# Two transformer models in a row: block 1's three in-layer norms without the sixteen idle products that TensorE issues in each

## The reference

```python
mod = silu(c) @ w_mod[l] + b_mod[l]
sh1, sc1, gt1, sh2, sc2, gt2 = jnp.split(mod, 6, axis=-1)
h = rms_norm(x, g_norm_mix[l]) * (1.0 + sc1) + sh1
x = x + gt1 * (attention(h @ w_in[l]) @ w_out[l])
h = rms_norm(x, g_norm_mlp[l]) * (1.0 + sc2) + sh2
x = x + gt2 * (jnp.square(jax.nn.relu(h @ w_mlp_in[l])) @ w_mlp_out[l])
```

## Time and profile before

| | us |
|---|---|
| median of 3 runs | 1664.45 (1663.45 to 1664.75) |
| the profiled execution's own time | 1665.32 |
| its span, from the first to the last instruction | 1663.4 |
| TensorE busy in the span | 1629.1 (98%) |
| VectorE busy | 1248.5 (75%) |
| ScalarE busy | 982.6 (59%) |

### The profile page before, as it was taken

How to read it: one execution, slowest core, us unless ns; L and a number is a source line. 1 busy time by engine, 2 the same in 40 slices (tenths; PEclk the granted TensorE clock), 3 DMA queues, 4 the chain that set the end, 5 groups by cost and what they waited for, 6 DMA issues and landing times.

```text
span 1663.4 us, 25160 instructions
## 1 busy us (share of the span) xinstructions
PE 1629.1 (98%) x9473; PEld 1364.3 (82%) x9473; DVE 1248.5 (75%) x1639; ACT 982.6 (59%) x1350; POOL 87.8 (5%) x105
## 2 busy tenths in 40 slices
PE   8999999999999999999999999999999999999998
PEld 6767888877777888899988888899978787887876
DVE  3876988877778665568676666568589988899887
ACT  4675544466754444546655545546667777677774
POOL 2150000004300000000000000000000000000000
PEclk9999999999999999999999999999999999999999
DMA  9757788845548565644355655554348999999995
GB/s 344 248 186 268 254 294 288 269 157 170 212 158 295 180 201 177 199 152 152 102 196 184 195 184 196 183 152 138 127 155 292 343 345 336 337 318 346 346 333 164
DMA packets 263287, 381.58 MB, mean 229 GB/s; under 512 B 8299, under 2 KB 197025, under 8 KB 263186
## 3 DMA queue, kind: packets, MB, share of 16 engines
q1 hardware_dynamic: 261520, 377.26, 68.5%
q0 software_dynamic: 1104, 1.76, 0.4%
q10 hardware_dynamic: 562, 1.18, 0.2%
HBM read 379.12 MB, written 1.05 MB: 229 GB/s over the span
## 4 chain that ended last, share of the span: by engine, by line
PE 82%; DVE 10%; ACT 4%; issue 1%; POOL 1%; DMA 1%; SPq 1%; DVEq 0%; ACTq 0%
PE bank L2285 55%; PE bank L2327 10%; PE bank L2329 5%; DVE w_low L1321 4%; ACT w_high L681 3%; PE bank L2375 3%; DVE mod_sums L1443 1%; PE bank L2884 1%; PE bank L2423 1%; DMA raw<-in_w_in_dram 1%; PE bank L2634 1%; SPq L462 1%; PE bank L2662 1%; DVE turned L1406 1%; DVE h_high_and_low L1391 0%
## 5 line engine op out<-in xcount | busy, mean ns | idle before, releaser
L1321 DVE TENSOR_TENSOR w_low<-raw,w_high 128x2048 fp32r<-128x2048 f32 (+2 forms) x315 | 689.4, 2192 | 178.7 <-ACT w_high L681 177.3
L681 ACT ACTIVATE w_high<-raw 128x2048 fp32r<-128x2048 f32 (+3 forms) x333 | 596.4, 1797 | 180.1 <-PE bank L2285 179.3
L2285 PE MATMUL bank<-w_high,h_high_and_low 128*128 128x512 f32 (+2 forms) x1536 | 485.3, 386 | 7.7 <-DVE w_low L1321 6.2
L2285 PEld LDWEIGHTS bank<-w_high,h_high_and_low 128*128 128x128 f32 x1536 | 285.4, 188 | 70.7 <-DVE w_low L1321 13.1
L2285 PE MATMUL bank<-w_low,h_high_and_low 128*128 128x512 f32 (+2 forms) x768 | 291.5, 380 | 0.0
L2327 PE MATMUL bank<-h_high_and_low,w_high 128*128 128x512 f32 x864 | 221.0, 394 | 2.9 <-DVE turned L2029 1.4
L2285 PE MATMUL bank<-w_high,act_high 128*128 128x512 f32 x544 | 213.6, 393 | 3.3 <-DVE act_low L1787 2.1
L2285 PE MATMUL bank<-w_low,act_high 128*128 128x512 f32 x544 | 211.6, 389 | 0.0
L2285 PE MATMUL bank<-w_high,act_low 128*128 128x512 f32 x544 | 211.2, 388 | 0.0
L2327 PEld LDWEIGHTS bank<-h_high_and_low,w_high 128*128 128x128 f32 x864 | 155.7, 188 | 33.9 <-issue 5.1
L2285 PEld LDWEIGHTS bank<-w_low,h_high_and_low 128*128 128x128 f32 x768 | 144.7, 188 | 24.0
(11 more groups left out here) (352 smaller groups left out, 1760.9 us busy)
## 6 DMA issues: line engine op xcount, KB each, us to landing
raw<-in_w_gu_exp_dram SPq DMA_DIRECT2D x160, 512.0 KB, 5.7
raw<-in_w_in_dram SPq DMA_DIRECT2D x52, 1024.0 KB, 5.3
raw<-in_w_mod_dram SPq DMA_DIRECT2D x48, 1024.0 KB, 5.5
raw<-in_w_dn_exp_dram SPq DMA_DIRECT2D x40, 1024.0 KB, 6.7
raw<-in_w_mlp_in_dram SPq DMA_DIRECT2D x32, 1024.0 KB, 5.6
raw<-in_w_mlp_out_dram SPq DMA_DIRECT2D x32, 1024.0 KB, 5.0
raw<-in_w_gu_dense_dram SPq DMA_DIRECT2D x22, 1024.0 KB, 5.1
raw<-in_w_out_dram SPq DMA_DIRECT2D x16, 1024.0 KB, 5.2
```

What stands on the lines that cost most here:

```text
L681: return nc.scalar.activation(dst, src, ACT.Copy, scale=scale)
L1321: V.tensor_tensor(wlo[w % SPLIT][:, 0:n], raw[raw_of(w) % RAW][:, 0:n], whi[w % SPLIT][:, 0:n].bitcast(F32), ALU.subtract).then_inc(raw_us ...
L2285: ins = T.matmul(out, lhsT, rhs, start=start and i == 0, stop=stop and i == len(pairs) - 1)
```

## The change

Eight lines of `turn_x` change: the choice of the idle bank and the three calls of `keep_busy`, for 2 + 2 + 5 + 7 = 16 products in each of norms 1, 2 and 3, are taken out. The transposes, their waits and `spread_rs` stay as they were and in their order. Norm 0 had no idle products here, since the calls stood behind `if n`. No other engine's list is touched.

```diff
         def turn_x(n, w, begin=0):
-            idle_bank = 7 if n % 2 else 4
             for i in range(begin, 4):
                 turn_quarter(n, i)
-                if n and i in (1, 2):
-                    keep_busy(2, idle_bank, w)
             if n:
-                keep_busy(5, idle_bank, w)
                 spread_rs(n)
-                keep_busy(7, idle_bank, w)
```

## The result

The changed kernel takes 1666.97 us in the median of 22 runs (1665.04 to 1668.86), and the kernel before, measured beside it, 1664.76 us (22 runs, 1663.19 to 1665.15). The ratio is 1.0015 with a 95% interval of 1.0009 to 1.0020: slower by 2.2 us. That is surely above nothing and just inside the 0.2% that the prediction had called the limit of what can be told from no change. The spread of its runs has grown too, from 2.0 to 3.8 us.

A forecast was written before the change was run, and what follows sets the result against it. TensorE was taken as the bound, busy 1629.1 of 1663.4 us. Gain 0, plus 1.15 us each in norms 1 and 3 and 1.45 in norm 2, made +3.75 us: median 1668.2, range 1667.0 to 1670.0 (8 in 10: 1663.8 to 1671.5).

The forecast's parts named there:

- The direct gain: Idle products of the three norms: removing them gains between 0 and 0.63 us; taken as 0.
- The clock falls in all three norms: New TensorE gaps of 1.6 and 2.25 us in each norm lower the clock; 2.5 to 5.5 us lost, chance 0.45.
- Rival 1: The clock holds through the norms' gaps: price 0, gain up to 0.63 us, 1663.8 to 1664.5 us; chance 0.25.
- rival 3: The clock stays down long, as over broken work at the start: 5.5 to 11.4 us lost; chance 0.11.
- rival 4: TensorE's queue was late after all and the spread comes sooner: near 1661 us; chance 0.02.
- How long it is down behind the restart: Once dense work begins again after a norm, the clock stays down 3.9 us; lower end near 1, upper 9 us.
- What that costs in norms 1 and 3: First products behind these norms: half of 3.9 us less 0.8 us slack, 1.15 us each.
- the slack: Time TensorE already loses waiting for the vector engine: 0.8 us behind norms 1 and 3, 0.5 us behind norm 2.
- Norm 2: First tile's products behind this norm: half of 3.9 us less 0.5 us slack, 1.45 us, all reaching the end.
- The spread at half rate: The spread's two transposes in each norm may run at half rate: up to 0.2 us a norm, taken as 0.
- rival 2: The clock falls in one or two norms, or rises again soon: 0.5 to 2.5 us lost; chance 0.17.

The follow-up runs named there:

- the transposes: Kernel before with the idle products of all three norms replaced by idle transposes of about the same time (5, 5, 12, 17): 1664.95 us, ratio 0.9999.
- the single removals: Kernel before with the sixteen idle products taken out of norm 1, 2 or 3 alone: 1665.88, 1665.68 and 1665.74 us.
- 21 idle products: Kernel before with 21 idle products instead of seven behind each spread: 1668.59 us, +3.76; behind norm 2's spread alone: 1665.41 us, +0.58.

## Why the prediction was right, and where it was off

- **The direct gain is nil: right.** The spread and the first product stand 0.06 and 0.14 us behind the vector engine's results, as they did. The work that hid the 48 products was the chain of squares, roots and first rests, and it is there without them.
- **The clock falls in all three norms: right.** PEclk was at 0.50 behind each, in the profile of the changed kernel. Rival 1, the clock holds, is out; so are rival 3 (in norms 1 and 3 the clock was back before the dense part) and rival 4. That the fall is the cause and not a bystander is shown by the transposes: they too take the idle products out, hold the clock, and cost nothing. It is shown a second time by the rows behind the restart, where a block takes 1.28 us while the clock is down and 0.70 us from 170.78 on, with the first product no later than before.
- **How long it is down behind the restart: near the mean, and partly by luck.** The forecast said 3.9 us, from the one rise at the start of the trace, which came under other work. It was 5.1 us in norm 1 (165.58 to about 170.7), 4.3 in norm 2 and 3.5 in norm 3 of one execution, and 6.1 in norm 2 of another. One value could at best be their mean.
- **What that costs in norms 1 and 3: right in the mean.** A block takes 1.28 us instead of 0.70, so 1 - 0.70/1.28 = 45% of the time at half rate is lost, less the slack. Norm 1: 5.1 x 0.45 - 0.84 = 1.5, measured 1.56 us. Norm 3: 3.5 x 0.45 - 0.84 = 0.7, measured 0.78 us. The forecast had 1.15 us for each; their mean was 1.17. By the medians of the single removals it was 0.99 and 0.85 us.
- **Norm 2 was mis-sized, and that is the step of the sum that failed.** The forecast took a slack of 0.5 us from the first tile's products and then said that "behind the norms TensorE is the bound, so what it loses there goes to the end". Behind norm 2 that is not so. In the kernel before, TensorE waits there for line 1321 at 367.15, and its products at 362.60 are stretched as well (0.73 us for two, where 0.54 is usual):

```profile
362.60 0.73 PE L2285 MATMUL bank<-w_high,h_high_and_low 128*128 128x416 f32 x2
...
367.15 0.53 PE L2285 MATMUL bank<-w_high,h_high_and_low 128*128 128x512 f32 x1 [0.49 <-DVE w_low L1321]
367.51 0.40 PE L2285 MATMUL bank<-w_low,h_high_and_low 128*128 128x512 f32 x1
```

In the changed kernel the same two places are these rows. TensorE comes later, finds the weights ready and waits for nothing:

```profile
365.05 0.54 PE L2285 MATMUL bank<-w_high,h_high_and_low 128*128 128x416 f32 x2
...
368.45 0.58 PE L2285 MATMUL bank<-w_high,h_high_and_low 128*128 128x416 f32 x2
368.87 0.40 PE L2285 MATMUL bank<-w_low,h_high_and_low 128*128 128x512 f32 x1
```

Counted from the spread, the pair of products is (365.05 - 354.84) - (362.60 - 353.86) = 1.47 us late, which is the forecast's 1.45. But the product at 367.51 is only (368.87 - 354.84) - (367.51 - 353.86) = 0.38 us late, and it stays so up to norm 3. So the loss in the first products was sized right, and 1.1 us of it were taken back where TensorE had waited anyway, which the forecast had left out: 0.49 us by the wait for line 1321, the rest at products that had stood further apart before, with no releaser named. With 21 idle products norm 2 forgave 2.48 - 0.63 = 1.85 us in all, not 0.5. Its term was thus 0.40 us in this profile, where the forecast had 1.45; in the kernel without norm 2's products alone it was 1.13 us in the profile and 0.79 in the median. In the profile this one term explains the step down from 3.75: the forecast's sum with 0.40 in it is 2.70, the marks give 2.74. The medians leave part of the step open. By the single removals norm 2 brings 0.66 us of the distance from 3.75 to 2.6, norms 1 and 3 bring 0.16 and 0.30, and intervals of 1.5 us to either side don't separate these.

- **The spread at half rate** was put at 0. It does happen where the fall comes early: 0.58 us in place of 0.43 in norm 2 of the changed kernel. It costs 0.15 us there.
- **The chances.** The measured 1666.97 us lies in the range for 8 in 10, and inside 0.2% of the kernel before, to which the prediction gave 0.54. The forecast itself had 2.5 to 5.5 us, and the +2.2 us lies just under it, in the range that rival 2 had by number. Rival 2's mechanism, a fall in one or two norms or an early rise, is not what the profile shows: the clock fell in all three and was down behind the restart for 4.3 us in the mean. The time also follows the clock from run to run: of the 22 runs of the changed kernel the nine with a mean granted clock of 0.994 took 1668.0 us in the mean, the six with 0.995 took 1666.8, and the seven with 0.996 took 1666.0. How long the half rate lasts and how much of it falls on wanted work differ from run to run, and with them the time.

What stays open is why the clock held in norm 1 with the nine idle products ahead of the spread and not in norms 2 and 3 of the same execution. Where the fall lies within a norm changes from execution to execution, and no run here sets it.

## What to carry to other kernels

A product that does nothing is free where TensorE waits anyway, and what it buys is read from the granted clock behind the wait, not from its busy time: look at PEclk, and at the distance between the first products after the restart. Put the idle work last, right ahead of the wanted work: seven products there did as well as sixteen as far as these runs can tell, while nine ahead of the spread lay 0.94 us above the kernel before, with a fall in two norms (its interval takes in no change too). Where the clock fell all the same, the half rate was spent wholly or in part on the seven. And price a delay by what waits behind it: about the same 2.4 us cost 1.5 us behind a norm that only TensorE bounds and 0.6 us behind one whose weights come late as well.

## What the runs showed of the hardware

- In the second profile of the kernel with seven products the clock fell in all three norms, and the mean granted clock of the execution was 0.995, a value that the changed kernel's runs have at 1666.8 us in the mean. This execution took 1665.08 us, against 1664.83 in the median of the kernel before. Its half rate fell on idle work, and for 1.4 and 0.6 us on wanted work that had that much to spare, so the mean granted clock by itself doesn't give the time.
- Transposes of 128x128 in float32 hold the clock at 2.4 GHz for a whole norm (PEclk 1.00, 158 to 166 us). Three products of 64 columns behind the spread, with gaps under 0.5 us between them, do not (PEclk 0.50 from 164.2 us).
